# A two-layer hybrid block and an expert layer on one core: the DVE order around attention, the split of a triangular solve, and two waits of ACT

## The reference

```
def hybrid_layer(x, ...):
    h = _rms(x) * norm1_g
    proj = h @ w_in                                  # 1024 x 7680
    aq, ak, av, rw, rq, rk, rv, rg, gates = _split(proj, IN_SIZES)
    aq = _rms(aq.reshape(B, T, ATTN_Q_HEADS, HEAD_DIM)) * attn_q_norm_g
    ak = _rms(ak.reshape(B, T, ATTN_KV_HEADS, HEAD_DIM)) * attn_k_norm_g
    o_a = sliding_window_attention(aq, ak, av, attn_sinks) @ w_attn_o
    o_b = rwkv7_time_mix(rw, ...) @ w_rwkv_o
    o_c = retention(rq, rk, rv, rg) @ w_ret_o
    g = jax.nn.sigmoid(gates).reshape(B, T, N_BRANCH, D)
    mixed = g[:, :, 0] * o_a + g[:, :, 1] * o_b + g[:, :, 2] * o_c
    x = x + mixed @ w_out
    ...
```

## Time and profile before

| | |
|---|---|
| median of three runs | 2351.78 us (2351.2 to 2353.42) |
| the profiled execution | 2351.2 us, span 2349.4 us |
| granted TensorE clock, mean | 0.918 of 2.4 GHz |
| busy over the span | PE 1919.0 us (82%), DVE 917.3 us (39%), ACT 505.1 us (21%), POOL 30.2 us (1%) |
| attention and tiles 19 to 29, layer 0 | from 133 to 230 us |
| the same in layer 1 | from 679 to 776 us |
| expert weights streaming | from 1400 us to the end, at 408 GB/s |

### The profile page before, as it was taken

One profiled execution on the slowest core, in us unless ns is written; L12 is line 12 of the kernel. 1 busy time (PEld: TensorE's weight loads), 2 busy tenths in 40 slices (PEclk: granted clock), 3 DMA queues, 4 the chain that ended last, 5 costly groups with the idle time before them and its releaser, 6 DMA issues.

```text
span 2349.4 us, 30387 instructions
## 1 busy us (share of the span) xinstructions
PE 1919.0 (82%) x13192; PEld 1372.5 (58%) x13192; DVE 917.3 (39%) x1238; ACT 505.1 (21%) x508; POOL 30.2 (1%) x23
## 2 busy tenths in 40 slices
PE   7999999999999999999999887556555665655655
PEld 6998789999999789999667662111111111111111
DVE  6688467556678558544356530000000000000001
ACT  3554023333555012332232020000000000000001
POOL 0000000000000000000000000000000000000000
PEclk9999999999999999999999988888888778788788
DMA  6444625656443725557323339999999999999997
GB/s 234 174 150 140 246 91 171 188 165 204 168 156 127 260 73 178 180 152 218 120 96 137 150 123 416 417 417 417 418 417 417 417 417 417 418 417 417 417 417 283
DMA packets 232087, 613.23 MB, mean 261 GB/s; under 512 B 11244, under 2 KB 106860, under 8 KB 198380
## 3 DMA queue, kind: packets, MB, share of 16 engines
q1 hardware_dynamic: 229760, 602.19, 67.6%
q10 hardware_dynamic: 2220, 9.45, 1.1%
HBM read 610.55 MB, written 1.05 MB: 260 GB/s over the span
## 4 chain that ended last, share of the span: by engine, by line
PE 51%; SPq 33%; DVE 7%; DMA 4%; issue 2%; ACT 1%; ACTq 0%; DVEq 0%; PEldq 0%
SPq L1401 32%; PE PS L1564 8%; PE PS L1557 8%; PE PS L1559 8%; PE PS L645 6%; PE PS L1509 3%; DMA ring<-in_w_gate 2%; PE PS L1587 1%; PE PS L1581 1%; PE PS L1582 1%; DMA work<-in_w_gate 1%; DVE ring_low L2238 1%; PE PS L1491 1%; PE PS L859 1%; PE PS L786 1%
## 5 line engine op out<-in xcount | busy, mean ns | idle before, releaser
L859 PE MATMUL PS<-work,proj 128*32 128x512 f32 x1024 | 162.7, 771 | 104.4 <-DMA work<-in_w_up 63.9
L1347 DVE TENSOR_TENSOR proj<-proj,PS 128x512 f32<-128x512 f32 x16 | 11.0, 687 | 512.6 <-PE PS L859 512.6
L859 PE MATMUL PS<-ring,proj 128*32 128x512 f32 x768 | 126.2, 790 | 89.2 <-DMA ring<-in_w_up 47.6
L2228 DVE TENSOR_TENSOR ring_low<-ring,high_f 128x4096 fp32r<-128x4096 f32 (+1 forms) x38 | 146.8, 3864 | 57.2 <-ACT high_f L2014 57.2
L2014 ACT ACTIVATE high_f<-ring 128x4096 fp32r<-128x4096 f32 (+1 forms) x38 | 120.8, 3179 | 220.8 <-PE PS L1564 204.2
L859 PEld LDWEIGHTS PS<-work,proj 128*32 128x32 f32 x1024 | 31.9, 127 | 227.1 <-DMA work<-in_w_up 105.0
L1557 PE MATMUL PS<-xh_f,high_f 128*128 128x256 f32 x640 | 153.6, 280 | 0.3 <-DVE xh_f L2249 0.2
L1559 PE MATMUL PS<-hT_low,high_f 128*128 128x256 f32 x624 | 151.1, 283 | 0.0
L645 PE MATMUL PS<-hT,ring 128*128 128x256 f32 (+1 forms) x576 | 131.3, 388 | 4.4 <-ACT hT L981 4.4
L859 PEld LDWEIGHTS PS<-ring,proj 128*32 128x32 f32 x768 | 24.4, 128 | 185.7 <-DMA ring<-in_w_up 77.3
L877 PE MATMUL PS<-work,proj 128*32 128x512 f32 x512 | 84.2, 792 | 59.5 <-DMA work<-in_w_down 56.7
(11 more groups left out here) (492 smaller groups left out, 3724.7 us busy)
## 6 DMA issues: line engine op xcount, KB each, us to landing
ring<-in_w_in SPq DMA_DIRECT2D x74, 1024.0 KB, 7.3
work<-in_w_gate SPq DMA_DIRECT2D x64, 1024.0 KB, 20.9
work<-in_w_up SPq DMA_DIRECT2D x64, 1024.0 KB, 26.8
work<-in_w_down SPq DMA_DIRECT2D x64, 1024.0 KB, 23.6
ring<-in_w_gate SPq DMA_DIRECT2D x48, 1024.0 KB, 22.4
ring<-in_w_up SPq DMA_DIRECT2D x48, 1024.0 KB, 26.7
ring<-in_w_down SPq DMA_DIRECT2D x48, 1024.0 KB, 18.5
ring<-in_w_ada SPq DMA_DIRECT2D x24, 1024.0 KB, 7.4
```

The costliest lines, as they stand in the source:

```text
L859: mm = nt.matmul(PS[32 * j:32 * j + 32, 2 + n // 4, :], x(k), w[:, F_E * kk + 512 * j:F_E * kk + 512 * (j + 1)], start=(k == 0), stop=(k = ...
L2228: nv.tensor_tensor(ring_low[:, n % RING, c], w, high(n)[:, c].bitcast(F32), ALU.subtract).then_inc(low_dve, 1)
```

## The change

Three edits, all within attention of both layers.

1. `SOLVED` goes from [8, 8, 14, 16, 18, 20, 31] to [10, 10, 14, 16, 22, 24, 31]. Read as stretches of `solve`, that is 8, 0, 6, 2, 2, 2, 11 steps before and 10, 0, 4, 2, 6, 2, 7 after. The total stays at 31.
2. `tile_highs` has no exception for tiles 23 and 24 any more: ACT waits for `block_done` of tile 21 before the high part of 23, and of tile 22 before that of 24.
3. On DVE only two of four diagonal blocks are gathered before the wait for `att_std`. The other two and `first_unknowns` come right after `att_rs`, ahead of the low parts of tile 21 and of `att_wide`; before, one diagonal block and `first_unknowns` came behind the low parts of tile 22.

```
-SOLVED = [8, 8, 14, 16, 18, 20, BLOCK - 1]
+SOLVED = [10, 10, 14, 16, 22, 24, BLOCK - 1]
...
-                    if q not in (23, 24):
-                        act.wait_ge(block_done, done(l, max(q - 2, 15) if q > 16 else 13))
+                    act.wait_ge(block_done, done(l, max(q - 2, 15) if q > 16 else 13))
                     if q == 23:
                         act.wait_ge(bonus_ss, 1)
                     if q == 24:
...
                 tile_lows(l, 20)
-                diagonal_blocks(0, 3)
+                diagonal_blocks(0, 2)
                 dve.wait_ge(att_std, 1)
                 link(nv.reciprocal(ATT_STAT, ATT_STAT))
                 widened(ATS, ATT_STAT).then_inc(att_rs, 1)
+                diagonal_blocks(2, P // BLOCK)
+                first_unknowns()
                 tile_lows(l, 21)
                 dve.wait_ge(att_wide, 1)
                 nv.scalar_tensor_tensor(q, q, ...).then_inc(att_qk, 1)
                 nv.scalar_tensor_tensor(kk, kk, ...).then_inc(att_qk, 1)
                 tile_lows(l, 22)
-                diagonal_blocks(3, P // BLOCK)
-                first_unknowns()
                 solve(0, SOLVED[0])
```

## The result

The changed kernel is slower: 2365.78 us median (2364.03 to 2367.66, 4 runs) against 2351.49 us (2349.81 to 2353.42, 4 runs), ratio 1.006 with a 95% interval of 1.0043 to 1.0078. It is slower, as forecast, but the predicted 2358.5 us was too low by 7.3 us, and the range ended at 2362.

The account below looks back on a forecast made before the run. In attention neither PE nor DVE was taken as full, so the order of waits decides. Layer 0's +4.3 and layer 1's +2.9, 7.3 with rounding, on the profiled 2351.2 gave 2358.5 us, range 2354 to 2362.

Parts of the forecast that it names:

- Direction, bound and hand-over: Whole kernel: slower by more than 0.2% (chance 0.80); what the attention layers lose is handed on one for one.
- DVE before round 0: Layer 0, DVE: transposes and unknowns moved ahead; round 0 could start at 172.4 instead of 170.91 us, 1.5 lost.
- tile 21: Layer 0, PE: its last eight matmuls wait for the low part, +1.66 us; tile ends at 167.03 instead of 165.37.
- the first new wait: Layer 0, ACT: high part of 23 waits for tile 21; the key copy comes later and PE's scores move +3.2 us.
- The second new wait: Layer 0, ACT: high part of 24 waits for tile 22, table load and exponential behind it; exponential +5.95 us.
- DVE alone: Rival: only DVE's idle time sets the attention layers' cost; together -2.7 us, 2348.5 us; chance 0.06.
- doesn't bind: Rival: ACT's second wait does not hold the exponential, only late scores remain; 2354.7 us; chance 0.10.
- no effect: Rival: ACT's added waits are already met, so the time stays; given no chance of its own.
- The schedule's sum, +4.3 in a layer: Layer 0: round 2 lags 5.65 us, PE gets back 1.3 at the end; line 1705 starts 4.3 us later.
- The unknown cost: the clock: PE, four new waits a layer of 1.4 to 2.2 us: clock loss 0 to 3.0 us in all, taken as nothing.
- the rival: PE's clock falls after the new waits, 1.5 to 3.0 us more: 2360.0 to 2361.5 us; chance 0.12.
- The sum is the same: Layer 1: +2.9 us; without the clock dip on tile 20 it loses 4.3 but saves the dip's 1.5.

Follow-up runs that it names:

- wait24_only: The kernel before with only the wait of the high part of 24 for tile 22 added; 2358.19 us median, ratio 1.0021.
- solved_only: The kernel before with only the new split of the solve (`SOLVED` as in the changed kernel); ratio 1.003.
- after_filled: The changed kernel plus two result-free 512-column matmuls on PE before the scores of round 0; 2362.51 us median, ratio 1.0038.
- after_filled_all: The changed kernel plus result-free matmuls before the scores of round 0 and before the transposes of rounds 0 and 2; 2364.92 us median, ratio 1.0045.
- after_again: The changed kernel itself, run again beside more runs of the kernel before; 2366.96 us against 2353.54, ratio 1.0059.
- waits_only: The kernel before with only the two ACT waits added, for tiles 21 and 22; 2364.05 us median against 2354.38, ratio 1.0041.

## Why the prediction was wrong

**Direction, bound and hand-over: right.** Nearly all of the profile's loss is made in the stretch and handed on: after line 1705 of layer 1 the executions take 1574.8 and 1574.9 us. That these two are so alike is in part luck: in the 12 other traces, whose kernels have no edit there either, the same stretch takes 1573.5 to 1580.1 us.

**DVE before round 0, tile 21, the first new wait: right.** Taken from the reciprocal, line 2490 starts at 8.47 us (163.59 less 155.12; forecast 8.34), round 0 at 17.81 (17.79), the scores at 15.80 (15.5).

**The second new wait, the mechanism: right.** The exponential stands behind high part and table load and no longer behind DVE. wait24_only shows the wait at work alone, +1.8 a layer. The rivals "DVE alone", "doesn't bind" and "no effect" fall.

**The schedule's sum, +4.3 in a layer: right.** With no dip on tile 22 or behind it, the changed order measured 78.71 and 78.72 against 74.20, +4.5.

**The step that failed is "The unknown cost: the clock", which took nothing.** The lower clock lay on tile 22 in both layers of both traced executions. In the first it added 1.5 us a layer (80.24 against 78.72), in the second 3.0 in layer 1. I held PE's new waits to be nearer to the 0.98 us that had left the clock alone than to anything the trace shows with a loss. That holds in the stretch, but not in the whole trace of before, which has, in the second block, PE waits of 2.61 and 2.99 us with a lower clock behind each, and one of 1.75 us without. So 2.25 lies 0.4 from a wait with a loss, and 1.3 from 0.98:

```profile
1212.60 1.49 PE L717 MATMUL PS<-proj,work 4*128 4x512 f32 x2 [2.61 <-ACT proj L1054]
1330.70 1.95 PE L623 MATMUL PS<-con,work 128*128 128x1 f32 x16 [2.99 <-DVE work L1266]
1340.51 10.63 PE L786 MATMUL PS<-hT,ring 128*128 128x256 f32 x48 [1.75 <-DVE hT L1235]
```

```profile
1213.00:1220.00 7.00, 7.00 (x14) 4.03 (x13) 2.90 (x6) 1.66 (x2) 0.00 (x0) 0.52 0.01 4
1330.00:1337.00 7.00, 6.30 (x29) 5.49 (x30) 0.85 (x2) 0.27 (x1) 0.00 (x0) 0.76 1.01 426
1337.00:1345.00 8.00, 6.25 (x34) 5.34 (x33) 1.66 (x4) 0.00 (x0) 0.00 (x0) 1.00 1.02 425
```

The first two waits end in smaller matmuls than those of tile 22, so they did not settle the price, but they spoke for the rival. The traces made afterwards do settle it. Of 14 stretches with a wait of 2.2 us on PE (before the scores, or before the low part of 23 in solved_only) the tile behind it ran slow in 10; behind waits of 0.98 us or less at those places, in none of 14. That the wait is the cause and not only beside it is shown by after_filled: same order, same start of the scores, only PE busy, and no dip on tile 22 in its two layers nor in the two of after_filled_all. With 4 of the 12 stretches that have the full wait before the scores free of a dip, four in a row would come by chance once in some 80 cases. By the Trainium skill (TensorE: Matmul & The Clock Gate, "HAM oscillation — how this bites in real kernels") gaps between bursts bring the clock down, in an example whose waits for DMA are longer than the 2.2 us here. The runs here agree on the cause, and show falls behind waits shorter than that section's: 2.2 us in 10 of 14.

**"The sum is the same", with or without the dip of tile 20: right, but not for the dip that came.** after_filled_all's layer 1 has the dip of tile 20 and takes 78.72 us like its layer 0, 3.0 more than the 75.69 of before (2.9 forecast). The changed kernel's layer 1 had no dip at tile 20 and one at tile 22, which the sentence has no price for. So the difference was 4.55.

**The range was too narrow, and the dips are not all of the miss.** Its upper case had one dip a layer, 2361.5 us; after_again's layer 1 had two. The profiled execution is 1.4 us above 2361.5: 0.9 is in the table's other rows, 0.3 in the two stretches, 0.2 outside the span. Such scatter of stretches that the change does not touch I had not looked for. The median of the timed runs is another 2.8 us above the profiled execution. So of the 7.3 us by which the forecast was low, the traces give 3.0 to the dips on tile 22 and 1.4 to the items above, and 2.8 have no trace. Which part of these is dips in untraced executions, and which is chance elsewhere, stays open.

## What to carry to other kernels

A wait added to an engine is paid by what is queued behind it, here a table load and an exponential, and not by the instruction that waits. When a schedule leaves PE idle for longer than any idle time in its stretch, look for waits of that length in the whole trace and see what the clock did behind them. Then price its fall at the tile that comes next, above all if that tile is on the path; work without a use that fills the wait is a cheap test and can be a cheap cure. Idle time of the leading engine is where moved work belongs: one transpose put into a 1.69 us wait, and a few steps into the next, gained 2.4 us a layer.

## What the runs showed of the hardware

- Behind a PE wait of some 2 us the granted clock falls in some executions and not in others. Counted over all 14 traces: waits of 1.66 to 1.68 us in tile 21, none of 11; 1.75 us before line 786, none of 14; 1.9 us before the transposes of round 0, 3 of 10; 2.2 us before the scores or before the low part of 23, 10 of 14; 2.6 us before line 717 and 3.0 us before line 623, 14 of 14 each. The work around these waits differs, so this is not a count by length alone.
- What the clock did just before goes with it: of the four stretches with a dip of tile 20 and the 2.25 us wait, one had the dip on tile 22 (waits_only); of the eight without, seven. Four are too few to call this a rule.
- Stretches without any change vary by more than a layer's difference between two orders. From the first product of the experts that reads `tri` (line 859) to the end, the 14 traces of this study took 950.6 to 951.1 us in eight cases and 953.0 to 953.7 us in six, nothing between, with no visible relation to the edits. From the last matmul of line 1705 to the first projection of the second block (line 645) they took 338.9 to 339.1, 340.6 to 340.8, or 342.4 us. The 70 timed runs of the kernel before reach from 2348.15 to 2356.98 us, the first four only from 2349.81 to 2353.42. What an edit of 0.2% does is seen far better in the traces, cut at common rows, than in a few timed runs.
- The table load of the exponential (1.28 us) does not wait for the activation's operands: before, it ran at 168.76 us for an exponential that started at 175.09; after, at 182.15, right behind the copies. It runs as soon as ACT's queue reaches it, and is free only as long as nothing ahead of it in the queue waits.
